# GLA level and diagonal products split at 64 tokens: four 64x64 array tiles in place of two 64x128 tiles

## The reference

```python
qf = q.astype(f32) * (DK ** -0.5)
b = jnp.cumsum(la.reshape(B, N, C, H, DK), axis=2)
causal = jnp.tril(jnp.ones((C, C), dtype=bool))[None, None, :, :, None, None]
dec = jnp.exp(jnp.where(causal, b[:, :, :, None] - b[:, :, None, :], -jnp.inf))
attn = jnp.einsum('bnihd,bnjhd,bnijhd->bnhij', qf, kf, dec)
o_intra = jnp.einsum('bnhij,bnjhv->bnihv', attn, vf)
```

## Time and profile before

| | before |
|---|---|
| median of 3 runs | 2264.63 us |
| lowest and highest | 2263.82 and 2267.15 us |
| span of the profiled execution | 2263.7 us |
| PE busy in it | 2224.6 us, 98% |
| PE loads busy | 1809.6 us, 80% |
| DVE busy | 1309.4 us, 58% |
| ACT busy | 897.3 us, 40% |
| granted clock of the matrix engine, mean | 0.999 of full |

### The profile page before, as it was taken

One profiled execution on the slowest core, in us unless ns is written; L12 is line 12 of the kernel. 1 busy time (PEld: TensorE's weight loads), 2 busy tenths in 40 slices (PEclk: granted clock), 3 DMA queues, 4 the chain that ended last, 5 costly groups with the idle time before them and its releaser, 6 DMA issues.

```text
span 2263.7 us, 39453 instructions
## 1 busy us (share of the span) xinstructions
PE 2224.6 (98%) x14668; PEld 1809.6 (80%) x14668; DVE 1309.4 (58%) x2870; ACT 897.3 (40%) x2015; POOL 105.2 (5%) x179
## 2 busy tenths in 40 slices
PE   8999999999999999999999999999999999999998
PEld 4778877788788888878877878777878888887877
DVE  4467655565376755646536776556645666654542
ACT  4444233353454333434425442244435542343321
POOL 1000000000000000000000000000000000000000
PEclk9999999999999999999999999999999999999999
DMA  7111212244211122324331121232441112241332
GB/s 250 32 57 29 57 38 66 66 147 139 85 39 30 43 64 74 72 77 137 132 89 44 29 52 43 52 96 78 141 135 42 44 30 64 48 103 38 97 110 75
DMA packets 230552, 172.08 MB, mean 76 GB/s; under 512 B 56886, under 2 KB 206908, under 8 KB 230332
## 3 DMA queue, kind: packets, MB, share of 16 engines
q1 hardware_dynamic: 226100, 154.78, 24.3%
q10 hardware_dynamic: 4264, 14.78, 1.9%
HBM read 136.60 MB, written 21.93 MB: 70 GB/s over the span
## 4 chain that ended last, share of the span: by engine, by line
PE 51%; DVE 1%; issue 1%; ACT 0%; DVEq 0%; ACTq 0%; POOLq 0%; POOL 0%
PE bank L1767 27%; PE bank L2814 13%; PE bank L1861 2%; PE bank L2071 1%; PE bank L2046 1%; PE bank L2022 1%; PE bank L2830 1%; PE bank L1839 1%; PE bank L2027 1%; PE bank L1845 1%; PE bank L1910 0%; PE bank L1814 0%; PE bank L1908 0%; PE bank L1934 0%; PE bank L1911 0%
## 5 line engine op out<-in xcount | busy, mean ns | idle before, releaser
L1767 PE MATMUL bank<-h_hi,w_hi 128*128 128x512 f32 (+3 forms) x2160 | 482.9, 361 | 15.1 <-issue 5.7
L1767 PE MATMUL bank<-h_lo,w_hi 128*128 128x512 f32 (+3 forms) x2160 | 484.6, 361 | 1.7
L1767 PE MATMUL bank<-h_hi,w_lo 128*128 128x512 f32 (+2 forms) x2080 | 462.5, 360 | 2.2
L1767 PEld LDWEIGHTS bank<-h_hi,w_hi 128*128 128x128 f32 (+1 forms) x2160 | 353.2, 186 | 90.7 <-issue 32.7
L1767 PEld LDWEIGHTS bank<-h_lo,w_hi 128*128 128x128 f32 (+1 forms) x2160 | 352.3, 185 | 72.7 <-issue 15.1
L1767 PEld LDWEIGHTS bank<-h_hi,w_lo 128*128 128x128 f32 x2080 | 345.3, 188 | 64.7 <-issue 12.9
L2814 PE MATMUL bank<-scr_r,tb_r 128*128 128x512 f32 x816 | 195.1, 395 | 1.0 <-issue 1.0
L2814 PEld LDWEIGHTS bank<-scr_r,tb_r 128*128 128x128 f32 x816 | 151.7, 188 | 35.6 <-issue 2.3
L2139 ACT ACTIVATE tb<-bank 128x512 f32<-128x512 f32 (+1 forms) x140 | 71.5, 510 | 226.2 <-PE bank L1767 217.3
L2295 ACT ACTIVATE scr<-bank 128x1024 f32<-128x1024 f32 x64 | 65.8, 1027 | 194.9 <-PE bank L2046 194.9
L2814 PE MATMUL bank<-w_hi,tb_r 128*128 128x512 f32 x544 | 136.1, 394 | 0.0
(11 more groups left out here) (299 smaller groups left out, 2928.1 us busy)
## 6 DMA issues: line engine op xcount, KB each, us to landing
w_raw<-in_w_in SPq DMA_DIRECT2D x96, 512.0 KB, 3.8
out<-scr SPq DMA_DIRECT2D x32, 512.0 KB, 2.7
scr<-in_w_out SPq DMA_DIRECT2D x16, 512.0 KB, 5.3
w_raw<-in_w_out SPq DMA_DIRECT2D x16, 512.0 KB, 3.6
scr<-in_x_prompt SPq DMA_DIRECT2D x16, 512.0 KB, 3.7
scr<-out SPq DMA_DIRECT2D x16, 512.0 KB, 3.4
rot<-out ACTq DMA_DIRECT2D x12, 512.0 KB, 3.7
mix_t<-in_x_prompt ACTq DMA_DIRECT2D x8, 512.0 KB, 14.9
```

The source lines that it names most:

```text
L1767: m = mm(bank[b][0:m_w, 0:c1 - c0], w[:, slot, k, 0:m_w], h[:, k, c0:c1], start=it["piece"] == 0 and k == 0, stop=it["piece"] == 2 and k = ...
```

## The change

Each of these products is cut at token 64 of the chunk. Both tokens of a pair that counts at a level below 64 lie in the same half of the chunk, so the level's product is now one for tokens 0 to 63 and one for tokens 64 to 127. Each has 64 stationary columns and 32 moving ones. The diagonal becomes two products of 64 by 64. The level v = 64 keeps one product per head, but with only the first 64 tokens as stationary columns. The result of the second half goes to partitions 64 to 127, which are the other 64 columns of the array. With two heads and two halves there are four tiles of 64x64. The costs in the forecast are changed as well, which can change the order of the items on every engine. The sample chunk (w = 64) has one half only and stays as it was.

```diff
         elif k == "gla_g":
-            p = run("PE", 0.33 if small else 0.88, self.needs(it))
+            p = run("PE", 0.33 if small else 0.45, self.needs(it))
...
         elif k == "gla_f":
-            p = run("PE", 0.49 if small else 1.22, self.needs(it))
+            p = run("PE", 0.49 if small else 0.68, self.needs(it))
...
                     last = [None, None]
-                    for h, hp in enumerate(heads):
-                        last[h] = mm(bank[4 + h][0:w, 0:w], k[hp], q[hp], start=True, stop=True)
+                    for j in range(w // HD):
+                        tk = slice(HD * j, HD * j + HD)
+                        for h, hp in enumerate(heads):
+                            last[h] = mm(bank[4 + h][tk, tk], k[hp, tk], q[hp, tk], start=True, stop=True)
                     for n, v in enumerate(levels):
                         if v < COARSE:
                             continue
                         x = e_row(s, 1 + n)[:, tok]
-                        for h, hp in enumerate(heads):
-                            last[h] = mm(compact(coarse_of(h, n), v), x[hp], pairs(x[hp], v)[:, :, 1, :],
-                                         start=True, stop=True)
+                        for j in range(w // (2 * v)) if v < HD else (0,):
+                            tk = slice(HD * j, HD * j + HD)
+                            to = slice(v * j, v * j + v)
+                            for h, hp in enumerate(heads):
+                                last[h] = mm(compact(coarse_of(h, n)[tk, to], v), x[hp, tk], pairs(x[hp], v)[:, j:j + 1, 1, :],
+                                             start=True, stop=True)
...
                     for j, (n, v) in enumerate(fine_of(s)):
                         x = e_row(s, 1 + n)[:, tok]
-                        for h, hp in enumerate(heads):
-                            m = mm(compact(bank[2 + h][0:w, j * w // 2:(j + 1) * w // 2], v), k[hp] if v == 1 else x[hp],
-                                   pairs(x[hp], v)[:, :, 1, :], start=True, stop=True)
-                            if v == 1:
-                                m.then_inc(bank_full[2 + h], 1)
+                        for i in range(w // HD):
+                            tk = slice(HD * i, HD * i + HD)
+                            o = j * w // 2 + HD // 2 * i
+                            for h, hp in enumerate(heads):
+                                m = mm(compact(bank[2 + h][tk, o:o + HD // 2], v), k[hp, tk] if v == 1 else x[hp, tk],
+                                       pairs(x[hp, tk], v)[:, :, 1, :], start=True, stop=True)
+                                if v == 1 and i == w // HD - 1:
+                                    m.then_inc(bank_full[2 + h], 1)
```

## The result

The changed kernel takes 2316.5 us (median of 4 runs, 2309.6 to 2318.6). Before it was 2265.0 us. The ratio is 1.022, with a 95% interval of 1.0206 to 1.0235. It is 51.5 us slower where 53 us faster were forecast.

A forecast was written before the change was run, and what follows sets the result against it. The matrix engine, busy 98% of the span, was taken to bound the kernel. 64 chunks saving 0.86 us give 55 us: 2263.7 - 55 + 3 = 2212 us; forecast alone 2204 to 2222, range extended to 2240.

The forecast's parts named there:

- The beat of a pass, four tiles at once, 1.07 us for a chunk: GLA products: loads set the beat, 0.058 us a pass for 0.1125; four tiles run together; a chunk takes 1.07 for 1.93.
- Rival 1: GLA products leave more slowly than four tiles can take them: 1.49 us a chunk, 2237 us in all; chance 0.13.
- The prediction's 2245: Total in us under rival 1 by the skill page: 60 cycles for each of 60 matmuls, 1.5 us a chunk.
- Rivals 3 and 4: GLA tiles sharing rows take turns, 2261 us, chance 0.02; supply runs dry after a burst, 2288 us, chance 0.04.
- I take 3 us of small new waits over the program, from bounds of 0 and 16: PE's added waits over the program; the upper bound is one wait of 0.25 us in each chunk.
- Rival 2: DVE or the new order makes PE wait 0.25 to 0.5 us a chunk: 16 to 32 us lost, 2226 to 2242; chance 0.09.
- The slack: Between chunks, from DVE's last copy to the next `gla_g`: 1.03 us, shrinking to about 0.2 as PE arrives 0.86 sooner.
- the planner, which knows the new costs, can put a further projection item of four matmuls there: Between GLA chunks, where the slack shrinks, one more projection item of 0.98 us could go.
- The slower rival: GLA's fine levels run slower once some 32 load and matmul pairs are used up: 2.29 us a chunk, 2288; chance 0.04.
- if the planner's new order opens waits far from GLA: One of two stated conditions for the prediction being wrong, about waits outside GLA; no size or chance given.
- the two full beats that the sum gave them: Level 64 in each full chunk: 2 passes on two tiles with half the stationary columns, at 0.058 us each.
- each bank is still signalled once per head, by its last product: GLA's banks: claimed that signalling stays as before and no wait is added, at no cost.

The follow-up runs named there:

- e1: Changed kernel (four 64x64 tiles) with the planner's costs of before, 0.88 and 1.22 us, so the old order; 2229.5 us, 0.984 of the kernel before.
- e7: e1 with two of DVE's five masked copies of a chunk (levels 16 and 8) left out, output not the reference's; 2214.3 us, 0.977.
- e5: Changed kernel with the new costs only in the first pass's plan, the costs of before in the second's; 2254.9 us, 0.995 of the kernel before.
- e6: Changed kernel with the new costs only in the second pass's plan, the costs of before in the first's; 2284.6 us, 1.008 of the kernel before.
- e11: Changed kernel with costs 0.55 and 0.80 in the first pass, 0.55 and 0.90 in the second, first-pass margin SAFE 0.3 for 0.5; 2219.3 us, 0.980.
- e2: Kernel before (two 64x128 tiles) with only the planner's new costs, 0.45 and 0.68 us; 2358.4 us, 1.040 of the kernel before.

## Why the prediction was wrong

- **The beat of a pass, four tiles at once, 1.07 us for a chunk: right.** Measured 1.05. The loads set the beat, it halved with their columns, and tiles that share rows load at the same time.
- **Rival 1, products leave too slowly: refuted.** 60 pairs of load and matmul start within 0.88 us, 15 ns a pair, below the 22.6 ns that the trace of before bounded. The 60 cycles for each matmul that "TensorEngine Tiling (Array Packing)" in the Trainium skill gives in its section Performance Considerations, an estimate of 25 ns at 2.4 GHz, do not add up over matmuls on different tiles here. (The prediction's 2245 for it has the fixed 0.13 us added to the 1.5, which it does not say.) Rivals 3 and 4, with 1.9 and 2.3 us for a chunk, are refuted by the 1.05.
- **A small misreading:** PE's waits for others before the change add up to 21 us, not to under 20. Nothing hangs on it.
- **"I take 3 us of small new waits over the program, from bounds of 0 and 16": this step failed.** It has two parts. In the old order the waits are 20 us (e1 against 2209), of which 15 go with 0.67 us of DVE work a chunk (e7). The prediction had the mechanism. Rival 2's 16 to 32 us were the right size for this part. The second part is two bullets below.
- **The slack was read at the wrong item.** Its 1.03 us go from DVE's last fine copy to the next `gla_g`, which needs banks 4 and 5. Those copies hold banks 2 and 3, for which `gla_f` waits. To `gla_f` the first chunk has 132.04 + 0.66 - 131.01 = 1.69 us. But `gla_f` also comes sooner by more than 0.86, since the next chunk's own `gla_g` shrinks from 0.66 to 0.29 us: 1.23 in all. That leaves 0.46, and e1 shows 0.44 there. Over the 48 pairs of neighbouring chunks in one slot, the kernel before has 1.6 us in the median and 0.97 at the least, less than 1.23. In e1, 20 of the 48 pairs have only the 0.26 us that pass from the copy's end at 214.54 to the load at 214.80. DVE itself falls behind as well: at 214.54 it is done 4.1 us after the products that it copies, and at the same place before it was 2.4 us.
- **The sentence "the planner, which knows the new costs, can put a further projection item of four matmuls there" was true, and was the larger fault.** It counted such an item as a cover that costs nothing. But the stock of projections is limited: 83 items in these three slots, before and after. What fills a gap in one slot is missing in a later one. The last GLA slot of the first pass fell from 28 items to 20, and its chunks then waited for DVE. With what else that list changes, it costs 25 us (e5). The attention over the samples in the second pass, far from GLA, fell from 5 items to none, and that list costs 55 us (e6). Together the new order costs 87 us (e1 to the changed kernel), about half of it idle time and half of it work at half clock.
- **The clock was not in the sum at all.** At 0.999 in the kernel before it looked like a constant. It was one as long as PE hardly paused. The profiles of e1 and the changed kernel put the price at 45.6 us, as much again as the new idle time.
- No rival ended on the slow side through the order of the work. The slower rival was a supply limit on the engine, and the edit of two numbers in the diff was not costed as a change of its own. That the prediction is wrong "if the planner's new order opens waits far from GLA" stood in the text, with no chance and no price.

What stays open: which single decision of the planner takes the items away from the second pass's attention, and how much of e6's 55 us that one place explains. Only whole lists were compared. For e11, costs and margin were not separated. That the clock falls because PE paused rests on what stands ahead of the slow stretches, and on e2, where it fell with the old tiles. No run filled a pause to see it stay up.

## What to carry to other kernels

A product whose time is the load of its stationary columns gets faster by cutting those columns onto tiles side by side, even when few moving columns are left. But where a planner orders the work from costs, a new cost is a second change, and must be tried apart from the first: here the better estimate of the costs made the worse list. Before calling a wait covered by filler work, count the filler that is left in the slots behind it, and price a pause of the matrix engine with the slow clock that follows it.

## What the hardware showed that was not expected

The tiles do not keep to one order. Level 64 uses only two of the four tiles, and the other two go on to the next products. In the changed kernel, products of L1869 start before the last ones of L1850, which stand ahead of them in the program. It is clearest in a chunk at half clock, and is the same in the first chunk by 4 ns:

```profile
262.64 0.48 PE L1850 MATMUL bank<-scr 64*64 64x64 f32 x10
262.88 0.30 PE L1869 MATMUL bank<-scr 64*64 64x32 f32 x2
262.93 0.30 PE L1850 MATMUL bank<-scr 64*64 64x32 f32 x2
262.99 0.98 PE L1869 MATMUL bank<-scr 64*64 64x32 f32 x28
```

So the two idle tiles of level 64 cost less than the two full beats that the sum gave them: in the first chunk, levels 64 and 32 take from 126.49 to 126.67 us, 0.18 in place of 4 x 0.058 = 0.23.

It has a second side. The product that signals a head's bank is the last one in the program, and no longer the last one to start. In the first chunk the two that signal banks 4 and 5 start at 126.638 and 126.645, and another of L1850 at 126.701. The signal then doesn't prove that the bank is complete. ACT reads these banks at 127.90 there, long after. In the chunk at 256.45, where ACT did wait for the signal, it starts at 257.03 and L1850's last matmul ends at 256.85. That is 0.18 us of room, the least of all 64 chunks, and nothing in the program guarantees it. Banks 2 and 3 are signalled in the same way. The prediction's "each bank is still signalled once per head, by its last product" is right of the program and not of the time.
